# Decay matrices of two sequence mixers: masks added in the matrix products, exponentials read from PSUM

## The reference, cut to what matters

```python
# GDN, one direction (gc: running sum of the log decay g; C = 64)
decay = jnp.exp(jnp.where(incl, gc[..., :, None] - gc[..., None, :], -jnp.inf))
lower = jnp.tril(jnp.einsum('nbhid,nbhjd->nbhij', kb, k) * decay, -1)
qk = jnp.einsum('nbhid,nbhjd->nbhij', q, k) * decay
# SSD, one direction (acum: running sum of dt * a)
X = xs * dt[..., None]
seg = jnp.exp(jnp.where(incl, acum[:, :, :, None] - acum[:, :, None, :], -jnp.inf))
cb = jnp.einsum('bclgn,bcsgn->bclsg', Cc, Bc)
y_diag = jnp.einsum('bclsgr,bcsgrp->bclgrp', cb[..., None] * seg, X)
# after both directions
y = (y + d_skip * xs) * jax.nn.silu(z); y = _rmsnorm(y, norm_w)   # per group of 8 heads
```

## Time and profile before

| | |
|---|---|
| median of three runs | 2286.61 us (2285.64 to 2288.24) |
| the profiled execution's own time | 2287.4 us |
| its span in the profile | 2285.2 us |
| busy in the span: PE, weight loads, DVE | 2172.6, 1976.9, 1547.2 us |
| busy in the span: ACT, POOL | 1332.4, 1112.2 us |
| mean granted clock of the tensor engine | 0.974 of full speed |

### The profile page before, as it was taken

One profiled execution on the slowest core, in us unless ns is written; L12 is line 12 of the kernel. 1 busy time (PEld: TensorE's weight loads), 2 busy tenths in 40 slices (PEclk: granted clock), 3 DMA queues, 4 the chain that ended last, 5 costly groups with the idle time before them and its releaser, 6 DMA issues.

```text
span 2285.2 us, 46234 instructions
## 1 busy us (share of the span) xinstructions
PE 2172.6 (95%) x14320; PEld 1976.9 (87%) x14320; DVE 1547.2 (68%) x3465; ACT 1332.4 (58%) x2706; POOL 1112.2 (49%) x883
## 2 busy tenths in 40 slices
PE   7989799999999999999898878999999999999998
PEld 6969699999999988888797557999999999888886
DVE  4776319985666577777767882199856665777776
ACT  6744355577777544444565664555777775444444
POOL 6851378987666600000176566779876775000000
PEclk9989899999999999999999888999999999999999
DMA  5510254555444566665544114545544445666664
GB/s 166 167 56 1 65 166 148 172 168 154 140 138 138 171 193 193 192 194 191 174 139 127 58 65 132 170 148 169 173 149 141 141 138 165 194 193 193 193 193 147
DMA packets 93891, 343.72 MB, mean 150 GB/s; under 512 B 10688, under 2 KB 10752, under 8 KB 93168
## 3 DMA queue, kind: packets, MB, share of 16 engines
q1 hardware_dynamic: 92592, 338.21, 47.2%
q0 software_dynamic: 928, 4.10, 0.6%
q10 hardware_dynamic: 288, 0.34, 0.0%
HBM read 341.56 MB, written 1.05 MB: 150 GB/s over the span
## 4 chain that ended last, share of the span: by engine, by line
PE 77%; POOL 7%; DVE 7%; issue 5%; ACT 3%; DMA 0%; POOLq 0%; DVEq 0%; ACTq 0%
PE bank L358 75%; POOL w_lo L1735 7%; DVE arena L1155 2%; DVE arena L1143 1%; DVE w_lo L890 1%; ACT w_hi L1376 1%; PE bank L378 0%; PE bank L521 0%; DMA small<-in_ssd_d 0%; ACT arena L1402 0%; ACT arena L1376 0%; DVE arena L863 0%; DVE arena L967 0%; DVE arena L988 0%; DVE arena L1198 0%
## 5 line engine op out<-in xcount | busy, mean ns | idle before, releaser
L1735 POOL TENSOR_TENSOR w_lo<-ring,w_hi 128x512 fp32r<-128x512 f32 x744 | 994.9, 1351 | 684.6 <-ACT w_hi L1376 672.3
L1376 ACT ACTIVATE w_hi<-ring 128x512 fp32r<-128x512 f32 x1280 | 801.9, 628 | 520.6 <-PE bank L358 518.9
L358 PE MATMUL bank<-hT_hi,w_hi 128*128 128x256 f32 x2688 | 780.5, 290 | 8.3 <-POOL w_lo L1735 6.3
L358 PE MATMUL bank<-hT_lo,w_hi 128*128 128x256 f32 x2688 | 761.7, 283 | 0.0
L358 PE MATMUL bank<-hT_hi,w_lo 128*128 128x256 f32 x2688 | 761.6, 283 | 0.0
L358 PEld LDWEIGHTS bank<-hT_hi,w_hi 128*128 128x128 f32 x2688 | 516.6, 192 | 19.3 <-POOL w_lo L1735 18.8
L358 PEld LDWEIGHTS bank<-hT_lo,w_hi 128*128 128x128 f32 x2688 | 517.0, 192 | 0.0
L358 PEld LDWEIGHTS bank<-hT_hi,w_lo 128*128 128x128 f32 x2688 | 516.1, 192 | 0.0
L890 DVE TENSOR_TENSOR w_lo<-ring,w_hi 128x512 fp32r<-128x512 f32 x536 | 377.2, 704 | 172.8 <-ACT w_hi L1376 167.6
L358 PE MATMUL bank<-w_hi,p_ag_hi 128*128 128x512 f32 x1024 | 398.4, 389 | 0.0
L358 PE MATMUL bank<-w_lo,p_ag_hi 128*128 128x512 f32 x1024 | 398.4, 389 | 0.0
(11 more groups left out here) (236 smaller groups left out, 2329.6 us busy)
## 6 DMA issues: line engine op xcount, KB each, us to landing
ring<-in_peer_u SPq DMA_DIRECT2D x256, 512.0 KB, 3.5
ring<-in_peer_v SPq DMA_DIRECT2D x256, 512.0 KB, 3.5
ring<-in_peer_wq SPq DMA_DIRECT2D x32, 512.0 KB, 3.5
ring<-in_gdn_qkv SPq DMA_DIRECT2D x24, 512.0 KB, 3.5
ring<-in_ssd_xbc SPq DMA_DIRECT2D x24, 512.0 KB, 3.5
ring<-in_ssd_z SPq DMA_DIRECT2D x16, 512.0 KB, 3.5
ring<-in_ssd_out SPq DMA_DIRECT2D x16, 512.0 KB, 3.5
ring<-in_gdn_z SPq DMA_DIRECT2D x8, 512.0 KB, 3.5
```

The lines of the kernel that those rows point to most:

```text
L358: return pe.matmul(o, w, r, start=first, stop=last)
L1376: return act.activation(o, i, ACT.Copy, scale=scale)
L1735: pool.tensor_tensor(w_part[1][:, s, :], ring[:, n % RING, hf * 512:(hf + 1) * 512], w_part[0][:, s, :].bitcast(F32), ALU.subtract).then_i ...
```

## The change

Both mixers. A mask tile is made on DVE in the convolution loop (`make_mask`): zero inside a triangle and -1e30 outside for each direction, zeros between, and a rounded identity. It lies in `p_ag[1]`; the high and low parts of the running sums now lie in 32 rows each of `p_ag[0]`, so one product with 64 rows replaces the two of 32 rows, and a second product adds the mask with the identity as weights. ACT takes the exponentials straight from PSUM, its bias being minus the token's own sum (for SSD plus the logarithm of dt, floored at 1e-37). Four exponentials per head replace one (GDN) or three (SSD).

SSD: each block of source tokens gets a bank of its own with 384 columns (four products a head instead of two). POOL adds the two directions, and a single DVE product of 128 x 512 with the unmasked C B matrices (`s_CB` has two blocks instead of three) gives the weights of a head. The skip term moves from ACT (one copy a head) to POOL (two products a group). The z projection leaves banks 6 and 7 by DVE copies (`gate_out`), except for the last group; its SiLU comes two heads into the next group, and the first `gate_half` of a group stands behind `spread` and `y_head`. `rows_out` and `rest_of_rows` move into the convolution loop.

GDN: both directions keep a matrix of their own (`g_E`, `g_Er`); DVE writes the query products for both directly; POOL adds the two system matrices after every second head before it masks level 0. `copy_predicated` and POOL's four masks of query products are gone.

```diff
-            def spread_row(bank, h, heads):
-                w = pick[0:heads, h:h + 1].to_broadcast([heads, P])
-                mm(bank[:, :], w, row[0][0:heads, :], True, False)
-                return mm(bank[:, :], w, row[1][0:heads, :], False, True)
+            def spread_row(bank, h):
+                mm(bank[:, :], pick[:, h:h + 1].to_broadcast([2 * SH, P]), s_row[:, :], True, False)
+                both = mask[:, 0:4 * P].rearrange("p (d o i) -> p d o i", d=2, o=2)[:, :, 0:1, :].to_broadcast([P, 2, NT, P])
+                return mm(bank[:, :].rearrange("p (d c i) -> p d c i", d=2, c=NT), mask[:, 3 * P:4 * P], both, False, True)
...
-                    spread_row(PS[h % 2], h, SH).then_inc(SEM["s_bc"], 1)
+                    for st in range(NT):
+                        o = PS[2 * (h % 2) + st][:, 0:3 * P]
+                        mm(o, pick[:, h:h + 1].to_broadcast([2 * SH, P]), s_row[:, st * P:(st + 3) * P], True, False)
+                        last = mm(o, mask[:, 3 * P:4 * P], mask[:, 0:3 * P], False, True)
+                    last.then_inc(SEM["s_bc"], 1)
...
                 for h in range(SH):
-                    gate_half(h)
+                    if h % SR:
+                        gate_half(h)
                     if h + 1 < SH:
                         spread(h + 1)
                     if h >= 2:
                         y_head(h - 2)
+                    if h % SR == 0:
+                        gate_half(h)
...
+            def make_mask():
+                dve.tensor_scalar(mask[:, 0:P], upper, 1.0, 1.0e30, ALU.subtract, ALU.mult).then_inc(SEM["masked"], 1)
+                dve.tensor_scalar(mask[:, P:2 * P], upper, 0.0, None, ALU.mult).then_inc(SEM["masked"], 1)
+                dve.tensor_scalar(mask[:, 2 * P:3 * P], lower, 1.0, 1.0e30, ALU.subtract, ALU.mult).then_inc(SEM["masked"], 1)
+                dve.tensor_copy(mask[:, 3 * P:4 * P], ident).then_inc(SEM["masked"], 1)
```

On DVE in the GDN heads `decay` goes, and the query products are written twice:

```diff
-                    dve.scalar_tensor_tensor(g_E[:, h, :], bank[:, T:2 * T], P ** -0.5, g_E[:, h, :], ALU.mult,
-                                             ALU.mult).then_inc(SEM["g_QE"], 1)
-                    if h % 2:
-                        s = slice(4 * (h // 2), 4 * (h // 2) + 4)
-                        dve.copy_predicated(g_AP[:, s, :], rows(levels[:, LEVELS, :].bitcast(mybir.dt.uint16), 4),
-                                            g_Af[:, s, :]).then_inc(SEM["g_A"], 1)
...
+                    dve.scalar_tensor_tensor(g_tok[:, :, h, :], kq, P ** -0.5, Ef, ALU.mult, ALU.mult)
+                    dve.scalar_tensor_tensor(g_PTb[:, h, :, :], kq, P ** -0.5, Er, ALU.mult, ALU.mult).then_inc(SEM["g_P"], 1)
```

On DVE in the SSD heads `decay` goes too, `weigh` is one product, and the z projection is copied out:

```diff
-                            last = dve.scalar_tensor_tensor(
-                                s_M[:, h % 2, st, d, :], s_CB[:, g, st, d, :], s_dt[:, st, d * SH + h:d * SH + h + 1],
-                                s_E[:, h % 2, st, d, :], ALU.mult, ALU.mult)
-                    last.then_inc(SEM["s_mv"], 1)
...
+                    dve.tensor_tensor(s_M[:, h % 2], s_CB[:, h // SR], s_E[:, h % 2, :, 0:2, :], ALU.mult).then_inc(SEM["s_m"], 1)
...
+                def gate_out(g):
+                    dve.wait_ge(half_used, 2 * (at[("sz", g, 3)] + 1))
+                    for t in range(NT):
+                        dve.tensor_copy(s_siluz[:, t, g * 512:(g + 1) * 512], PS[6 + t][:, :]).then_inc(SEM["s_zraw"], 1)
...
                 for h in range(SH):
-                    decay(h)
-                    if h:
-                        gate_rest(h - 1)
-                        weigh(h - 1)
-                    if h > SR and h % SR == 3:
-                        group_out(h // SR - 1)
+                    gate_rest(h)
+                    if h % SR == SR - 1 and h < SH - 1:
+                        gate_out(h // SR)
+                    weigh(h)
+                    if h >= 6 and h % 4 == 2:
+                        four_out(h // 4 - 1)
```

ACT and POOL in the SSD heads:

```diff
-                    act.activation(s_E[:, h % 2, 0, 2, :], PS[h % 2][:, P:2 * P], ACT.Exp, bias=s_nac[:, 0, h:h + 1])
-                    act.activation(s_E[:, h % 2, 1, 2, :], PS[h % 2][:, T:T + P], ACT.Exp, bias=s_nac[:, 1, SH + h:SH + h + 1])
...
-                    act.activation(v, v, ACT.Exp).then_inc(SEM["s_e"], 1)
...
-                    copy(s_skip[:, :, o], s_tok[:, :, o], s_D[:, h:h + 1]).then_inc(SEM["s_skip"], 1)
+                    act.activation(flat(e[:, 0, 0:2, :], "s i"), b0[:, 0:2 * P], ACT.Exp, bias=s_nac[:, 0, h:h + 1])
+                    act.activation(e[:, 0, 2, :], b0[:, 2 * P:3 * P], ACT.Exp, bias=s_nac[:, 0, SH + h:SH + h + 1])
+                    act.activation(e[:, 1, 0, :], b1[:, 0:P], ACT.Exp, bias=s_nac[:, 1, h:h + 1])
+                    act.activation(flat(e[:, 1, 1:3, :], "s i"), b1[:, P:3 * P], ACT.Exp, bias=s_nac[:, 1, SH + h:SH + h + 1]
+                                   ).then_inc(SEM["s_e"], 1)
...
-                m = s_M[:, h % 2]
-                pool.tensor_tensor(m[:, :, 0, :], m[:, :, 0, :], m[:, :, 1, :], ALU.add).then_inc(SEM["s_m"], 1)
+                e = s_E[:, h % 2]
+                pool.tensor_tensor(e[:, :, 0, :], e[:, :, 0, :], e[:, :, 2, :], ALU.add).then_inc(SEM["s_sum"], 1)
+                if h % SR == 1:
+                    skip(h // SR)
```

More of the change, by code:

```diff
@@ L248, in hybrid_encoder @@
         s_E = take(2, NT, 3, P)
-        s_M = take(2, NT, 3, P)
+        s_M = take(2, NT, 2, P)
         s_junk = take(512)
@@ L281, in hybrid_encoder @@
         p_act = take(2, T)
-        row = [flat(p[0:SH, :, :], "s t") for p in p_ag]
-        pick = sb("pick", [SH, SH], F32R)[:, :]
+        row = [flat(p_ag[0][i * SH:(i + 1) * SH, :, :], "s t") for i in range(2)]
+        pick = sb("pick", [2 * SH, SH], F32R)[:, :]
+        s_row = flat(p_ag[0][0:2 * SH, :, :], "s t")
+        mask = flat(p_ag[1][:, :, :], "s t")
         x_loaded, small_loaded, gain_loaded = sem("x_loaded"), sem("small_loaded"), sem("gain_loaded")
@@ L953, in gdn @@
                         dve.tensor_tensor(flat(g_gt, "t c"), PS[3][:, 32:64], flat(g_gc, "t c"), ALU.subtract).then_inc(SEM["g_cumsb"], 1)
+                        dve.tensor_scalar(g_z, g_gc, -1.0, None, ALU.mult).then_inc(SEM["g_minus"], 1)
+                    if m == 7:
+                        dve.tensor_scalar(p_ag[0][0:2 * SH, 1, :], flat(const[0:2 * SH, 0:2, :], "m i"), 0.0, None, ALU.mult)
+                    if m == 12:
+                        make_mask()
                     if m == 14:
-                        rest_of_rows(0, GH)
+                        rest_of_rows(0, GH, row[1][0:GH, :])
                 tok_copy(10)
@@ L1103, in gate_output @@
                     dve.scalar_tensor_tensor(s_da, s_dt, -1.0, rows(s_nega, NT), ALU.mult, ALU.mult).then_inc(SEM["s_da"], 1)
+                    dve.tensor_scalar(s_z, s_dt, 1.0e-37, None, ALU.max).then_inc(SEM["s_floor"], 1)
                 def tok_copy(gi):
@@ L1122, in ssd @@
                         dve.wait_ge(SEM["s_cum"], 1)
-                        link(dve.tensor_copy(flat(s_ac, "t c"), PS[3][:, 0:128]))
-                        dve.tensor_scalar(s_nac, s_ac, -1.0, None, ALU.mult).then_inc(SEM["s_nac"], 1)
-                rest_of_rows(1, SH)
+                        dve.tensor_copy(flat(s_ac, "t c"), PS[3][:, 0:128]).then_inc(SEM["s_cumsb"], 1)
+                    if m == 12:
+                        make_mask()
+                    if m == 14:
+                        rest_of_rows(1, SH, s_row[SH:2 * SH, :])
@@ L1134, in ssd @@
[L1134 to L1145 removed]
+                    v = PS[6 + g % 2][:, :].rearrange("p (q i) -> p q i", i=P)
@@ L1492, in gdn @@
                 for h in range(GH):
-                    act.wait_ge(SEM["g_logE"], h + 1)
-                    act.activation(g_E[:, h, :], g_E[:, h, :], ACT.Exp).then_inc(SEM["g_E"], 1)
+                    act.wait_ge(SEM["g_bc"], h + 1)
+                    for d, E in enumerate((g_E, g_Er)):
+                        for c in range(NT):
+                            last = act.activation(E[:, h, c * P:(c + 1) * P], PS[h % 2][:, (2 * d + c) * P:(2 * d + c + 1) * P],
+                                                  ACT.Exp, bias=g_z[:, c, d * GH + h:d * GH + h + 1])
+                    last.then_inc(SEM["g_E"], 1)
                     if h < 4:
```

189 lines of the change are left out of this document (81 added, 108 removed).

## The result

The changed kernel takes **2266.22 us** (median of four runs, 2266.17 to 2268.4) against 2286.97 for the kernel before: ratio 0.9912, 95% interval 0.99 to 0.9924. 2263 was predicted, with 2249 to 2276 as its range. The profiled execution has a span of 2266.6 us, 18.6 less than before (its own time, 2268.4 us, is the longest of the four).

What follows compares the result with a forecast made beforehand. DVE was taken to bound the SSD heads, and PE after the change. Gains of 9.4 (loop), 8.9 (tail) and 7 (GDN), less 1 (convolutions), sum to 24.3 us off 2287.4: 2263 us, range 2249 to 2276.

Steps and rivals of the forecast that it cites:

- PE becomes the bound, 3.75 us a head: SSD heads: DVE, ACT and POOL all stay below PE, whose work grows from 3.14 to 3.75 us a head.
- Two more changes of shape, 0.38: SSD heads on PE: four array shape changes a head instead of two, 0.19 us for each added one.
- Rival B: SSD heads: the two more shape changes cost nothing, 3.37 us a head, 2251 us in all; chance 0.20.
- Loop gain 9.4: SSD head loop, first spread to last gate half: 115.7 us instead of 125.13, a gain of 9.4.
- Rival D: SSD heads: PE's clock falls to half, 6.8 us a head; with 11 such heads about 2297 us; chance 0.06.
- So PE's 3.79 us waits go: SSD group ends: PE's 3.79 us waits for ACT's SiLU vanish, and with them the half clock.
- Tail gain 8.9: From the last SSD gate half to the first transpose: 10.4 us instead of 19.35, a gain of 8.9.
- GDN gain 7: GDN heads without gate units (4 to 7) through mask_y: a gain of 7 us, bounds 5 and 9.
- about 5.2: GDN mixer: time from the first extend to mask_y, about 5.2 us instead of 5.88.
- Convolution cost 1: Convolutions: making the masks on DVE costs 1 us for both mixers, bounds 0 and 4.
- The worst case: Convolutions: four mask operations at 1.25 us each with POOL at work, 5 us a mixer at most.
- Rival C: SSD heads: something else, DVE and POOL blocking or ACT's SiLU, holds them at about 4 us; 2274 us; chance 0.18.

Runs made afterwards that it cites:

- e2: Changed kernel with pick filled up to 128 rows with zeros, so no change of array shape in either mixer's heads: 2239.2 us, ratio 0.9794.
- e11: Kernel before the change, with both SSD spreading products taking 128 rows (pick filled with zeros): 2284.31 us, ratio 0.9987.
- e1: Changed kernel with each SSD head's two 64-row products first, then both 128-row mask products: 2249.05 us, ratio 0.984.
- e3: Changed kernel with the old group end: SiLU straight from banks 6 and 7, no DVE copies, gate half first: 2265.59 us, ratio 0.991.
- e5: Changed kernel with a group's first gate half ahead of spread and y_head again, DVE copies kept: 2263.89 us, ratio 0.9898.
- e9: Changed kernel with POOL's add and level mask of the last GDN batch moved to DVE, between second and third extend: 2265.87 us, ratio 0.9909.
- e4: Changed kernel with the four mask-making DVE operations issued three times in the first mixer instead of once: 2267.96 us, ratio 0.9922.
- e7: e2 with the SSD mask product on only the two blocks with a triangle, 256 columns instead of 384: 2235.89 us, ratio 0.9776.
- e8: e2 with the group end as before the change (the edit of e3): 2246.81 us, ratio 0.9821.

## Why the prediction was right, point by point

The median was forecast to 3 us, and the reading of the bottleneck was right. The sum was less good: 24.3 us of gain were forecast, the profiled execution has 18.6 and the medians 20.8. Two terms were too large, one mechanism was put down to the wrong part, and one of the prediction's own signs of being wrong came true: the clock fell in the loop.

- **PE becomes the bound, 3.75 us a head.** Right: 3.76, no wait of PE in the loop, DVE 7.94 of 18 us busy (the prediction's 1.8 us of 3.75 is 48%, measured 44%). That the hundredth agrees is luck: spreading takes 1.40 us and not the 1.28 forecast, `y_head` 0.81 and not 0.91.
- **Two more changes of shape, 0.38.** Right in kind: e2 gives 0.195 each. The size came out by luck in part. It was worked out from products of 32 rows, by taking all the excess of 0.37 us a head in the earlier trace rows for the two changes; e11 shows that only 0.23 of it goes when they are gone, 0.115 each. The 64-row products happened to cost more. The other part, 384 columns at the plain rate, is what e2 shows when the changes are gone. Rival B (they cost nothing) is out by e1 and e2. The Trainium skill's rule (TensorEngine Tiling (Array Packing), Key Properties), that changing the tiling mode drains the engine, agrees with the 0.195 us a change; e1 adds that the order of products sets how often it is paid.
- **Loop gain 9.4.** Mis-sized: 6.1 (119.0 us instead of 115.7). The missing 3.3 us are the stretch at half clock. Rival D named such a mechanism, a clock that falls with PE's excess around the shape changes, but as all or nothing; one stretch of 6.5 us came. What I took from the earlier trace rows against it, that gaps of 9% had not hurt, did not bear on eight changes in a row.
- **"So PE's 3.79 us waits go", because the gate half moves and DVE copies.** The waits went, but not for that: with all of this undone (e3) they are 0.8 us and the clock stays up. The cause, as the traces have it, is that `decay` no longer holds ACT. The sum did not suffer, as the heads were counted at PE's pace either way; but at this pace of PE the six copies and the reordering buy nothing (e3), and the gate half's new place costs about 2 us by the traces (e5).
- **Tail gain 8.9.** 8.5: the three `y_head` and the chain behind them took 10.8, not 10.4; PE waited 0.32 us for the last `weigh`.
- **GDN gain 7.** Mis-sized: 6.0 from the first spread on, and 5.0 in place, since 1.0 went in front of it, where the transposes ran at half clock, as they did in e11 without the change. First extend at 149.8 (149.4 forecast): heads 4 to 7 begin 0.9 us later than assumed, and their spreads are 1.74 apart instead of the 1.95 taken for DVE, so two errors cancel there. The step that failed is "about 5.2" from there to `mask_y`: it took 7.7. I had only asked when the last batch would come, not what POOL's add and mask do to DVE's extends beside them: 3.96 us for the first two instead of 2.07. With POOL idle (e9) the way from extend to `mask_y` is 5.6 us, near the 5.2. Between `mask_y` and the output transposes 0.9 us came back (85.7 us instead of 86.7), which the prediction put at nothing; no run shows from what.
- **Convolution cost 1.** Not contradicted: a set costs 0.5 to 1 us by the medians of e4, or nothing that they can tell; that the changed kernel still comes to the scaling 0.4 us earlier than the one before lies within the scatter of 3 us between profiles. The worst case, four locks of 1.25 us, was one lock a set here. The Trainium skill's rule (SBUF — State Buffer, Who interferes with whom), read as "each of them waits for one POOL operation", would have been too dear by a factor of three. The rows agree with the lock itself, held for a whole operation: 1230 against 216 ns, the extends, and in e4 two operations in a row of 1320 ns where POOL did not pause. How many wait depends on POOL's pauses, which the prediction did not ask for.
- **Not in the sum**: 1.0 us lost after the SSD mixer. PE runs at half clock behind the 6 us wait in both kernels, from 1355.06 for about 9.4 us and before from 1374.67 for about 8.4. Half of that difference is lost, 0.5 us; the rest stays open.
- **Rival C** (something else holds the heads at 4 us) is out: no waits. It would be next at 2.9 us a head, as e7 shows.

## What to carry to other kernels

A product with fewer rows than its neighbours is cheap in columns and dear in changes of shape: fill it up with zero rows, or put products of one shape side by side, as soon as PE sets the pace; before that it buys little (2.5 us in e11, 27.0 in e2). When a chain through DVE is taken out, waits elsewhere that look like a matter of order may go with it, so undo each companion edit by itself before it is kept. And an engine that the profile calls busy can still be slow: read the granted clock next to the busy share.

## What was new about the hardware

- A change between 64 and 128 rows cost 0.195 us (e1, e2), and one between 32 and 128 rows with 512 columns about 0.1 (0.23 a head for two, e11 against before).
- The granted clock fell to 0.50 for 6.5 us while PE was busy in all of it, behind two spreads and two `y_head` with eight changes of shape; it did so in all four profiles with that sequence, once each and at one of three such places; in the loops of the other seven it fell once, behind a wait of 1.9 us (e8).
- The extends (DVE, 128 x 512, both inputs in SBUF) took 1.03 us each with POOL idle and up to 2.09 beside POOL's add and mask. Of four short DVE operations in a row only the first was held up where POOL paused behind it, and the third and fourth as well (1.32 us each) where POOL did not.
